# Two-block network on one core: gates of the recurrence split over two levels, norm spreads over the full height, and doubling steps that move only the columns they change

## Chip, cores and metric

One core of a Trainium2 chip. The metric is the device time of one launch in microseconds (us); the median of several runs counts. Everything is float32.

## What is computed

The reference is two transformer blocks behind one another, with 256 tokens of 1024 values. The first block has two layers of a convolutional mixer, cross attention and a feed-forward part (one of them a mixture of eight experts). The second has an attention layer and an RWKV-7 layer, each followed by a squared-ReLU feed-forward part. The change lies in the RWKV layer, whose heart is a recurrence over the tokens, for 16 heads and two directions:

```python
def rwkv7_scan(r, w, k, v, kk, a):
    def step(state, inp):
        r_t, w_t, k_t, v_t, kk_t, a_t = inp
        sa = jnp.einsum('bhvk,bhk->bhv', state, -kk_t)
        state = (state * w_t[:, :, None, :] + sa[..., None] * (kk_t * a_t)[:, :, None, :]
                 + v_t[..., None] * k_t[:, :, None, :])
        return state, jnp.einsum('bhvk,bhk->bhv', state, r_t)
```

The keys `kk` are normalised for each head: `kk / max(sqrt(sum(kk * kk)), 1e-12)`. A gate `g = sigmoid(xg @ g1) @ g2` for each direction multiplies the normalised output of the recurrence.

## The kernel before

The network is written engine by engine. Each engine has its own queue, executed in order; semaphores tie them together, and every wait is written out by hand.

The recurrence (`chunks`) doesn't step through tokens. It takes two chunks of 128 tokens (the time tiles, `t` = 0, 1) and solves a triangular system of 128 x 128 for each. It works on eight *pairs* of heads (128 channels), and in each on two directions `d`. The triangular matrix is inverted by doubling in blocks of 64: level `k` (0 to 5) joins blocks of 2^k rows to blocks twice as large. A pair has four such matrices for each direction (two tiles, two heads, index `n`), and each consists of two corners `b` in the two halves of the partitions. Two kinds of the inverse are kept, itself and its transpose, side by side in one tile `XX` of 2 x 4 x 64 columns: the regions.

A level of one direction goes like this:

- `halves` (L3783): TensorE multiplies `GM` by the kind-0 part of `XX`, eight matmuls of 64 x 64 by 64 columns, into bank `A(d)`.
- `take_half` (L3602): ScalarE copies the 256 columns of the product to `Pb`.
- `steps` (L3796): TensorE multiplies with `Pb`, for both kinds (only kind 1 in level 5), sixteen matmuls of 64 x 64 by 64 columns.
- `step` (L4069): VectorE copies what is fresh into `XX` with `copy_predicated`. In a level only every second block of 2^k columns changes, in kind 0 the even ones and in kind 1 the odd ones; the views `moved` and `places_of` pick these 128 columns of each region, in runs of 2^k, from `XX` and from the result in PSUM.

Each float32 matmul appears in the trace as two records. TensorE's queue runs level by level and, in it, direction 0 and then 1: half products, a filler, steps. The filler is other work of the pair: transposed rows and the Gram products `rest` (L3730, L3733) in levels 1 and 2, the `gates` (L3745, L3746) of both tiles in level 3, nothing in level 4, and the right-hand sides (L3770, L3771) in level 5. Then come the two substitutions (`solve_first`, `carry`, `solve_second`, `state`, `right_sides`, `outputs`), between them the first products of the next pair (`m1`, `gram`).

```python
for d in range(2):
    halves(i, k, d)
    ...
    elif k == 3:
        gates(i, d)
    elif k == LEVELS - 1:
        right_sides(i, 0, d)
    steps(i, k, d)
```

VectorE's queue (`pair`) puts between the levels' steps, in a fixed order, the masking of the Gram products (`keep_rest`, L4061), the pieces of `factors(i + 1)`, which make the operands of the next pair (L3983 to L4004), and the pieces of `output(i - 1)`, which finish the former pair (L4019 to L4045). The product L4002 in `factors` waits until the gates of this pair are done, since it overwrites `rkd`, which they read. ScalarE's queue has `take_half` of each level and between them the exponentials of the next pair, the gates' copy (`take_gates`, L3612) and the normalisation of the former pair (`normalise`, L3618, four for each direction; that of direction 1 stands ahead of level 5). GpSimd makes the reciprocal roots for it.

Ahead of the recurrence, `gates_and_keys` spreads the inverse norms of the 16 heads to all channels. `outof` is a matrix of 16 rows (heads) by 1024 columns, and `scale` has the 16 x 256 inverse norms: eight matmuls (L3390) with 16 rows, each of 256 moving columns, into five banks in turn. VectorE multiplies each by its keys (L3409) and then makes the operands of the first pair for both directions (L3211 to L3218). Behind the spreads TensorE runs the 16 matmuls of the gates' first factor (L3393), and ScalarE applies the sigmoid (L3402). The stage ends, for all engines, with the last of them.

Of the kernel before, what the change touches and what calls it, by code (L numbers as in the profile page):

```python
# [24 lines left out]
P = 128  # L25
SEQ = 256
# [3037 lines left out]
def rwkv_constants():  # L3064
# [17 lines left out]
    rows_of_heads = np.ascontiguousarray(heads_of_rows.T.reshape(KC, P, D // HEAD).transpose(1, 0, 2))  # L3082
    return {"kept_places": np.stack(keep).astype(np.float32), "level_places": np.stack(level).astype(np.int32),
# [3 lines left out]
class Rwkv:  # L3087
# [50 lines left out]
    def place_low(self, ctx):  # L3138
# [3 lines left out]
        self.outof = tmp(ctx, "out_of_heads", [D // HEAD, D])  # L3142
# [77 lines left out]
    def project(self, gain):  # L3220
        m = self.m
        nc, x = m.nc, m.xT
        with ExitStack() as inner:
# [4 lines left out]
            scale = tmp(inner, "scale", [D // HEAD, SEQ])  # L3228
# [57 lines left out]
            def clear_state(pool):  # L3286
                for d in range(2):
                    pool.memset(self.S0[d][:], 0.0)
                pool.memset(self.gn_eps[:], GN_EPS).then_inc(self.cleared.sem, 1)
# [21 lines left out]
            self.low_rank(mixed[0], self.a1, a_low, ACT.Copy, self.a2, "a0", self.rate, mixing(5, mixed[1]), scale=scale)  # L3311
# [3 lines left out]
    def low_rank(self, x, w1, low, func, w2, bias, dst, extra, squares=None, scale=None):  # L3315
# [7 lines left out]
        with m.block() as block:  # L3323
# [20 lines left out]
            def _(act):  # L3344
# [3 lines left out]
                if scale is not None:  # L3348
                    act.wait_ge(summed.sem, summed.at(1))
                    act.activation(scale[:], ps[0:D // HEAD, 1, 0:SEQ], ACT.Sqrt).then_inc(rooted.sem, 1)  # L3350
# [8 lines left out]
            def _(dve):  # L3359
                extra(dve, chain)  # L3360
                if scale is not None:
                    dve.wait_ge(rooted.sem, rooted.at(1))
                    chain.link(dve.tensor_scalar(scale[:], scale[:], 1e-12, None, ALU.max))
                    dve.reciprocal(scale[:], scale[:]).then_inc(inverted.sem, 1)
# [11 lines left out]
    def gates_and_keys(self, x, g1, low, k, scale, kk, places):  # L3376
# [39 lines left out]
    def chunks(self, ctx, y, into, gain, loads):  # L3416
# [82 lines left out]
        def both_kinds(d):  # L3499

            return ps[:, A(d):B(d) + 1, :].rearrange("p a b -> p (a b)")[:, 4 * HEAD:]

        def made(d, kind, n):

            at = n * HEAD
            if region(kind, d):
                return ps[:, B(d), at:at + HEAD]
            return ps[:, A(d), 4 * HEAD + at:4 * HEAD + at + HEAD]
# [39 lines left out]
        with m.block() as block:  # L3548
# [14 lines left out]
            def _(pool):  # L3563
# [655 lines left out]
```

## Time and profile before

| | |
|---|---|
| median of 3 runs | 2555.06 us (2554.2 to 2559.51) |
| the profiled execution | 2555.09 us, span 2553.4 us |
| TensorE (PE), busy share of the span | 96% |
| TensorE weight loads (PEld) | 83% |
| VectorE (DVE) | 43% |
| ScalarE (ACT) | 19% |
| GpSimd (POOL) | 7% |
| stage of gates and keys | about 2030 to 2044.5 us |
| recurrence, eight pairs | about 2045 to 2313 us |

The profile comes from one execution. A row of the timeline has the start in us from the span's start, the time from the first start to the last end of the merged instructions, engine, line, operation, the tiles (out<-in), shapes and count, and in brackets the idle time of the engine before it with what ended it. A matmul's shape is "stationary rows*columns moving". A row of the windows has the window and its length, then busy us and instructions of PE, PEld, DVE, ACT and POOL, then the granted share of TensorE's clock (1.00 is 2.4 GHz, 0.50 is 1.2 GHz), the DMA share and GB/s. A row of the waits has the waiting instruction, what it waited for, us in total, times and the longest. A row by line and shape has the count, busy us and mean ns of one, then idle time before.

### The profile page before, as it was taken

The numbers are of one execution on the slowest core, as the hardware profiler recorded it, in microseconds if no ns is written. First come the engines' busy times: TensorE is split into PE (matmuls) and PEld (weight loads), VectorE is DVE, ScalarE is ACT, GpSimd is POOL, SyncE is SP. The second block draws the span as 40 slices with busy tenths as digits, with TensorE's granted clock in tenths as the row PEclk, the third lists the DMA queues.
The fourth block names the chain that finished last, engine by engine and source line by source line (L and its number), as shares of the span: only waits on it lengthen the run. The fifth ranks groups of instructions, "written<-read, shape, count | busy, mean of one in ns | idle before, by whom it ended". The sixth has DMA issues, their size and how long they took to land. (4 is left out here: it accounts for less than half of the span.)

```text
span 2553.4 us, 80275 instructions
## 1 busy us (share of the span) xinstructions
PE 2461.7 (96%) x36143; PEld 2113.9 (83%) x36143; DVE 1086.1 (43%) x2659; ACT 477.5 (19%) x1062; POOL 179.1 (7%) x225
## 2 busy tenths in 40 slices
PE   9999999999999999999999999999999989989998
PEld 7898878789879989999999898777768777778775
DVE  5672554477321010110101102446664478866666
ACT  2112000211132323210000001310010455542000
POOL 0100000010022322210000000000000001110000
PEclk9999999999999999999999999999999999989999
DMA  7444554554589999999999999326565000020453
GB/s 239 156 143 144 170 164 132 170 180 149 203 312 407 407 407 408 407 407 405 407 407 407 407 407 341 112 90 201 202 204 167 1 9 8 7 71 26 167 178 116
DMA packets 289906, 571.11 MB, mean 224 GB/s; under 512 B 18190, under 2 KB 180244, under 8 KB 289764
## 3 DMA queue, kind: packets, MB, share of 16 engines
q1 hardware_dynamic: 289764, 569.10, 61.1%
q8 instruction: 103, 1.69, 0.3%
q14 instruction: 39, 0.32, 0.0%
HBM read 567.98 MB, written 5.28 MB: 225 GB/s over the span
## 5 line engine op out<-in xcount | busy, mean ns | idle before, releaser
L2688 PE MATMUL ps<-xg,ring 128*64 128x80 f32 x14336 | 507.5, 233 | 7.0 <-issue 5.6
L2688 PEld LDWEIGHTS ps<-xg,ring 128*64 128x64 f32 x14336 | 500.9, 137 | 12.3 <-issue 8.5
L2811 DVE TENSOR_TENSOR hidden<-acted,ps 128x320 f32<-128x320 f32 x64 | 28.5, 446 | 659.8 <-PE ps L2688 659.8
L2704 PE MATMUL ps<-hidden,expert_down 128*64 128x80 f32 x7168 | 257.8, 234 | 9.3 <-issue 3.9
L2704 PEld LDWEIGHTS ps<-hidden,expert_down 128*64 128x64 f32 x7168 | 252.7, 138 | 11.7 <-issue 8.9
L2753 ACT ACTIVATE ring<-second 128x1792 f32<-128x1792 f32 x60 | 101.9, 1698 | 210.0 <-PE ps L2688 190.9
L639 PE MATMUL ps<-xT,ring 128*128 128x256 f32 (+1 forms) x592 | 131.4, 381 | 0.4 <-PEq L474 0.4
L639 PEld LDWEIGHTS ps<-xT,ring 128*128 128x128 f32 (+1 forms) x592 | 105.9, 181 | 23.7 <-issue 3.5
L2745 POOL COPY ring<-second 128x1792 f32<-128x1792 f32 x60 | 100.9, 1681 | 307.9 <-PE ps L2688 183.8
L639 PE MATMUL ps<-ring,xT 128*128 128x256 f32 (+1 forms) x544 | 108.9, 361 | 2.2 <-PEq L1144 2.2
L639 PEld LDWEIGHTS ps<-ring,xT 128*128 128x128 f32 x544 | 96.0, 190 | 14.5 <-issue 3.0
L2046 PEld LDWEIGHTS ps<-xT,ring 128*128 128x128 f32 x720 | 87.4, 192 | 14.3 <-issue 9.1
L2081 PE MATMUL ps<-ring,hidden 128*128 128x512 f32 x192 | 92.9, 593 | 0.0
L2046 PE MATMUL ps<-xT,ring 128*128 128x128 f32 x720 | 90.2, 275 | 0.4 <-DVE made L2165 0.4
L2760 ACT ACTIVATE acted<-ps 128x320 f32<-128x320 f32 x64 | 22.4, 401 | 353.9 <-PE ps L2688 353.5
L2016 ACT ACTIVATE S<-u 128x512 f32<-128x512 f32 x8 | 5.0, 630 | 392.2 <-DVE u L2221 389.2
L1763 PE MATMUL ps<-ring,hidden 128*128 128x512 f32 x176 | 77.2, 592 | 0.0
L1047 DVE SCALAR_TENSOR_TENSOR conv<-gated,cols,conv 128x256 f32<-128x256 f32 x180 | 71.4, 477 | 0.0
L2081 PE MATMUL ps<-wT,hS 128*128 128x512 f32 x128 | 65.4, 593 | 0.0
L639 PE MATMUL ps<-second,ring 128*128 128x256 f32 x288 | 63.8, 379 | 0.0
L1763 PEld LDWEIGHTS ps<-ring,hidden 128*128 128x128 f32 x176 | 32.7, 190 | 37.3 <-issue 37.3
L2046 PE MATMUL ps<-T,S 128*128 128x128 f32 x480 | 63.4, 275 | 0.0
(662 smaller groups left out, 3929.1 us busy)
## 6 DMA issues: line engine op xcount, KB each, us to landing
expert_down<-in_moe_w_down_dram SPq DMA_DIRECT2D x96, 1024.0 KB, 16.8
ring<-in_mlp_w_dram SPq DMA_DIRECT2D x64, 1024.0 KB, 5.4
ring<-in_moe_w_gate_dram SPq DMA_DIRECT2D x68, 896.0 KB, 15.9
ring<-in_moe_w_up_dram SPq DMA_DIRECT2D x68, 896.0 KB, 16.4
second<-in_moe_w_gate_dram SPq DMA_DIRECT2D x30, 1792.0 KB, 17.4
second<-in_moe_w_up_dram SPq DMA_DIRECT2D x30, 1792.0 KB, 18.8
ring<-in_w_xkv_dram SPq DMA_DIRECT2D x16, 1024.0 KB, 5.5
expert_down<-in_moe_w_down_dram SPq DMA_DIRECT2D x32, 512.0 KB, 16.2
```

The lines of the kernel that those rows point to most:

```text
L639: mm = pe.matmul(bank(n, dst), left(here), right(here), start=(i == 0), stop=(i == len(pairs) - 1))
L1047: ins = dve.scalar_tensor_tensor(conv[:, i, :], gated[:, i, k:k + SEQ], w, conv[:, i, :], ALU.mult, ALU.add)
L1763: mm = pe.matmul(ps[:, 4 + 2 * t + half, :], hidden[:, p, f, t * P:(t + 1) * P], w[:, f, half * 512:(half + 1) * 512], start=first and f = ...
L2016: act.activation(junk[:, 0:512], half_of(dst, t, half), ACT.Square, accum_out=part[:, t, half:half + 1]).then_inc(squares_summed.sem, 1)
L2046: mm = pe.matmul(to, left[:, c, :], right[:, c, :], start=(c == 0), stop=(c == H - 1))
L2081: return pe.matmul(to, left, right, start=first, stop=last, skip_group_check=True)
L2688: mm = pe.matmul(bank[b][o:o + HEAD, at, :], w[:, c, f * P + o:f * P + o + HEAD], xg[:, p * E_STEP + c, :], start=(p == 0 and c == 0 and a ...
L2704: mm = pe.matmul(yT[c // 4][o:o + HEAD, c % 4, :], w[:, j, c * P + o:c * P + o + HEAD], hidden[:, f, :], start=False, stop=False, skip_gro ...
L2745: pool.tensor_copy(self.expert_in(1, p), self.expert_waiting(1, p, 1)).then_inc(loaded[1][p], 16)
L2753: act.activation(self.expert_in(0, p), self.expert_waiting(0, p, 1), ACT.Copy).then_inc(loaded[0][p], 16)
L2760: act.activation(acted[:, part, :], src, ACT.Silu).then_inc(act_done, 1)
L2811: dve.tensor_tensor(hidden[:, part, :], acted[:, part, :], src, ALU.mult).then_inc(hidden_ready, 1)
```

## The change

- The gates of a direction are split by time tile: tile 0 is the filler of level 3, tile 1 that of level 4.
- `halves` moves only the 32 columns of each 64 that the level changes, and its results are packed (32 columns for each matrix). `take_half` copies 128 columns instead of 256 and writes them, in runs of 2^k, to the changing places of `Pb`; the rest of `Pb` is cleared once, by GpSimd, ahead of the first pair. `steps` moves 32 columns as well; its results are packed, 128 for each kind, and VectorE reads them contiguously. The stationary operands keep their 64 columns.
- The normalisation of direction 1 is cut in two parts, which stand behind level 4's first copy and between the copies of the gates; the gates' copies move between the copies of levels 4 and 5.
- The norm spreads take all 128 rows: `outof` and `scale` get 112 rows of zeros. They no longer stand ahead of the gates' matmuls but between them, one behind each from the fifth of direction 0 to the fourth of direction 1.

```diff
@@ gates_and_keys, tensor
-                for c in range(KC):
-                    if c >= SPREAD:
-                        pe.wait_ge(taken.sem, taken.at(c - SPREAD + 1))
-                    pe.matmul(ps[:, 3 + c % SPREAD, 0:SEQ], self.outof[:, c * P:(c + 1) * P], scale[:], start=True, stop=True).then_inc(spread.sem, 1)
                 for d in range(2):
                     for c in range(KC):
                         mm = pe.matmul(ps[:, 2 * d, 0:SEQ], g1[:, c, d, :], x[:, c, :], start=(c == 0), stop=(c == KC - 1))
+                        if d == 0 and c >= 4:
+                            e = c - 4
+                            pe.matmul(ps[:, 3 + e, 0:SEQ], self.outof[:, e * P:(e + 1) * P], scale[:], start=True, stop=True).then_inc(spread.sem, 1)
+                        elif d == 1 and c < 4:
+                            e = c + 4
+                            if e >= SPREAD:
+                                pe.wait_ge(taken.sem, taken.at(e - SPREAD + 1))
+                            pe.matmul(ps[:, 3 + e % SPREAD, 0:SEQ], self.outof[:, e * P:(e + 1) * P], scale[:], start=True, stop=True).then_inc(spread.sem, 1)
@@ chunks
+        PART = HEAD // 2
-        def both_kinds(d):
-            return ps[:, A(d):B(d) + 1, :].rearrange("p a b -> p (a b)")[:, 4 * HEAD:]
+        def both_kinds(d, k):
+            packed = ps[:, A(d):B(d) + 1, :].rearrange("p a b -> p (a b)")[:, 12 * PART:20 * PART]
+            return packed.rearrange("p (r n m b) -> p r n m b", r=2, n=4, b=1 << k)
+        def changing(block, k, kind, d):
+            return block.rearrange("p (m z b) -> p m z b", z=2, b=1 << k)[:, :, region(kind, d), :]
@@ gpsimd
+                pool.memset(Pb[0][:], 0.0)
+                pool.memset(Pb[1][:], 0.0).then_inc(self.cleared.sem, 1)
@@ scalar, take_half
-                    act.activation(Pb[d][:].rearrange("p a b -> p (a b)"), ps[:, A(d), 0:4 * HEAD], ACT.Copy).then_inc(q["half_ready"].sem, 1)
+                    to = changing(Pb[d][:].rearrange("p a b -> p (a b)"), k, 0, d)
+                    act.activation(to, ps[:, A(d), 0:4 * PART].rearrange("p (m b) -> p m b", b=1 << k), ACT.Copy).then_inc(q["half_ready"].sem, 1)
@@ scalar, pair
-                    take_halves(i, 4)
-                    for d in range(2):
-                        take_gates(i, d)
+                    take_half(i, 4, 0)
                     if not first:
-                        normalise(i - 1, 1)
-                    take_halves(i, 5)
+                        normalise(i - 1, 1, range(2))
+                    take_half(i, 4, 1)
+                    take_gates(i, 0)
+                    if not first:
+                        normalise(i - 1, 1, range(2, 4))
+                    take_half(i, 5, 0)
+                    take_gates(i, 1)
+                    take_half(i, 5, 1)
@@ tensor, halves
-                            mm = pe.matmul(ps[other, A(d), n * HEAD:(n + 1) * HEAD], GM[d][h, n, 0, h], XX(i, d, 0, n)[h], start=True, stop=True)
+                            mm = pe.matmul(ps[other, A(d), n * PART:(n + 1) * PART], GM[d][h, n, 0, h], changing(XX(i, d, 0, n)[h], k, 0, d), start=True, stop=True)
@@ tensor, steps
-                                mm = pe.matmul(made(d, kind, n)[on], p if kind else xt, xt if kind else p, start=True, stop=True)
+                                mm = pe.matmul(made(d, kind, n)[on], p if kind else xt, changing(xt if kind else p, k, kind, d), start=True, stop=True)
@@ tensor, pair
-                            elif k == 3:
-                                gates(i, d)
+                            elif k < LEVELS - 1:
+                                gates(i, k - 3, d)
@@ vector, step
-                    x, fresh, places = moved(XXs[d][i % 2][:], k), moved(both_kinds(d), k), places_of(k)
+                    x, fresh, places = moved(XXs[d][i % 2][:], k), both_kinds(d, k), places_of(k)
```

## Rows read from the trace of the kernel before

**Rows 1.** Busy time by window: one middle pair of the recurrence.
```profile
2144.70:2176.80 32.10, 29.39 (x759) 24.47 (x759) 25.75 (x80) 17.94 (x54) 3.25 (x8) 1.00 0.03 7
```

**Rows 2.** Who waited for whom, in the same pair.
```profile
ACT Pb L3602 <- PE ps L3783: 9.9, 8, 1.7
...
DVE XX L4069 <- PE ps L3796: 0.7, 2, 0.5
```

**Rows 3.** Timeline of TensorE, levels 3 and 4 of that pair.
```profile
2153.43 0.63 PE L3783 MATMUL ps<-XX,GM 64*64 64x64 f32 x16
...
2157.55 0.63 PE L3783 MATMUL ps<-XX,GM 64*64 64x64 f32 x16
...
2158.67 0.27 PE L3796 MATMUL ps<-Pb,XX 64*64 64x64 f32 x2 [0.49 <-ACT Pb L3602]
...
2160.83 0.63 PE L3783 MATMUL ps<-XX,GM 64*64 64x64 f32 x16
```

**Rows 4.** Timeline of ScalarE, same pair, level 5.
```profile
2160.69 1.43 ACT L3618 ACTIVATE o<-o,rs 128x64 f32<-128x64 f32 x4
...
2162.01 0.38 ACT L3602 ACTIVATE Pb<-ps 128x256 f32<-128x256 f32 x1
```

**Rows 5.** Timeline of VectorE, same pair, levels 1 to 4.
```profile
2148.45 0.72 DVE L4069 COPY_PREDICATED XX<-level,ps 128x256 f32<-128x256 int32 x1
...
2154.71 0.95 DVE L4061 TENSOR_TENSOR GM<-ps,keep 128x768 f32<-128x768 f32 x1
...
2155.85 0.43 DVE L4069 COPY_PREDICATED XX<-level,ps 128x256 f32<-128x256 int32 x1 [0.19 <-PE ps L3796]
...
2157.22 0.41 DVE L3997 TENSOR_TENSOR front<-r,front 128x256 f32<-128x256 f32 x1
...
2157.90 0.43 DVE L4069 COPY_PREDICATED XX<-level,ps 128x256 f32<-128x256 int32 x1 [0.27 <-issue]
...
2158.97 0.42 DVE L4004 TENSOR_TENSOR front<-kd,eB 128x256 f32<-128x256 f32 x1
...
2159.91 0.43 DVE L4069 COPY_PREDICATED XX<-level,ps 128x256 f32<-128x256 int32 x1 [0.53 <-PE ps L3796]
```

**Rows 6.** Timeline of TensorE outside the recurrence, for the spacing of matmuls.
```profile
86.75 1.03 PE L639 MATMUL ps<-xT,ring 128*64 128x256 f32 x4
...
87.71 2.44 PE L955 MATMUL ps<-vnorm,wsT 128*128 128x64 f32 x20
...
2401.55 1.61 PE L2046 MATMUL ps<-xT,ring 128*128 128x128 f32 x13
```

**Rows 7.** Groups by line and shape, recurrence: a ScalarE copy of 128 elements.
```profile
L3624 ACT ACTIVATE rhs<-ps 64x128 f32<-64x128 f32 x32 | 8.7, 271 | 22.0 <-PE ps L3775 21.6
```

**Rows 8.** Timelines of TensorE, VectorE and ScalarE, stage of gates and keys.
```profile
2029.99 5.66 PE L3390 MATMUL ps<-scale,out_of_heads 16*128 16x256 f32 x16 [1.14 <-PEq L3323]
...
2035.69 0.48 DVE L3409 SCALAR_TENSOR_TENSOR xT<-k,cols,ps 128x256 f32<-128x256 f32 x1 [0.37 <-PE ps L3390]
...
2040.57 0.41 DVE L3218 TENSOR_TENSOR front<-dn 128x256 f32<-128x256 f32 x1
...
2044.15 0.38 ACT L3402 ACTIVATE g_low<-ps 128x256 f32<-128x256 f32 x1 [3.07 <-PE ps L3393]
```

**Rows 9.** Busy time by window again, for the granted clock (PEclk).
```profile
918.80:922.20 3.40, 3.40 (x58) 3.40 (x56) 0.00 (x0) 0.00 (x0) 0.00 (x0) 0.50 1.04 412
...
2031.50:2038.40 6.90, 6.90 (x18) 4.99 (x17) 5.92 (x16) 4.27 (x11) 0.00 (x0) 0.51 0.00 0
...
2161.20:2164.70 3.50, 2.68 (x74) 2.13 (x69) 3.36 (x12) 2.38 (x8) 0.00 (x0) 1.00 0.00 0
```

**Rows 10.** Timeline of TensorE, last pair, half products of levels 2, 3, 5.
```profile
2282.85 0.56 PE L3783 MATMUL ps<-XX,GM 64*64 64x64 f32 x12 [2.54 <-issue]
...
2285.12 1.06 PE L3783 MATMUL ps<-XX,GM 64*64 64x64 f32 x16
...
2297.44 0.79 PE L3783 MATMUL ps<-XX,GM 64*64 64x64 f32 x16
```

More of the change, by code:

```diff
@@ L3141, in place_low @@
         self.into = tmp(ctx, "into_heads", [P, KC, D // HEAD])
-        self.outof = tmp(ctx, "out_of_heads", [D // HEAD, D])
+        self.outof = tmp(ctx, "out_of_heads", [P, D])
         self.loaded = self.m.sig("rwkv_tables_loaded")
@@ L3227, in project @@
             w_low, a_low = tmp(inner, "w_low", [P, SEQ]), tmp(inner, "a_low", [P, SEQ])
-            scale = tmp(inner, "scale", [D // HEAD, SEQ])
+            scale = tmp(inner, "scale", [P, SEQ])
+            by_head = scale[0:D // HEAD, :]
             def mixing(n, dst):
@@ L3288, in clear_state @@
                     pool.memset(self.S0[d][:], 0.0)
+                pool.memset(scale[:], 0.0)
                 pool.memset(self.gn_eps[:], GN_EPS).then_inc(self.cleared.sem, 1)
@@ L3349, in _ @@
                     act.wait_ge(summed.sem, summed.at(1))
-                    act.activation(scale[:], ps[0:D // HEAD, 1, 0:SEQ], ACT.Sqrt).then_inc(rooted.sem, 1)
+                    act.wait_ge(self.cleared.sem, self.cleared.at(1))
+                    act.activation(scale, ps[0:D // HEAD, 1, 0:SEQ], ACT.Sqrt).then_inc(rooted.sem, 1)
                 act.wait_ge(low_done.sem, low_done.at(1))
@@ L3362, in _ @@
                     dve.wait_ge(rooted.sem, rooted.at(1))
-                    chain.link(dve.tensor_scalar(scale[:], scale[:], 1e-12, None, ALU.max))
-                    dve.reciprocal(scale[:], scale[:]).then_inc(inverted.sem, 1)
+                    chain.link(dve.tensor_scalar(scale, scale, 1e-12, None, ALU.max))
+                    dve.reciprocal(scale, scale).then_inc(inverted.sem, 1)
                     dve.wait_ge(self.cleared.sem, self.cleared.at(1))
@@ L3612, in take_gates, with normalise @@
                     act.activation(gb(i, d)[:], ps[:, G(d), 0:SUMS + 4], ACT.Copy).then_inc(q["gates_ready"].sem, 1)
-                def normalise(j, d):
+                def normalise(j, d, ns=range(4)):
                     wait(act, "gn_rstd", j, d + 1)
                     ov = o[d][:].rearrange("p (n e) -> p n e", n=4)
-                    for n in range(4):
+                    for n in ns:
                         a = act.activation(ov[:, n, :], ov[:, n, :], ACT.Identity, bias=rs[d][:, 2, n:n + 1], scale=rs[d][:, 1, n:n + 1])
-                    a.then_inc(q["normed"].sem, 1)
+                    if n == 3:
+                        a.then_inc(q["normed"].sem, 1)
                 def take_right(i, s, d):
@@ L3693, in _ @@
                     take_m1(0, d)
+                act.wait_ge(self.cleared.sem, self.cleared.at(2))
                 for i in range(pairs):
@@ L3739, in rows, with gates @@
                     mm.then_inc(q["rows_done"].sem, 1)
-                def gates(i, d):
-                    wait(pe, "slice_loaded", i, 32)
-                    wait(pe, "rest_kept", i, 2 + d + 1)
-                    for t in range(TT):
-                        pe.matmul(ps[:, G(d), t * P:(t + 1) * P], g_low[:, d, t * P:(t + 1) * P], g2[:, d, :], start=True, stop=True)
-                        mm = pe.matmul(ps[:, G(d), SUMS + 2 * t:SUMS + 2 * t + 2], rkd[d][:, t, :], head_of, start=True, stop=True)
-                    mm.then_inc(q["gates_done"].sem, 1)
+                def gates(i, t, d):
+                    if t == 0:
+                        wait(pe, "slice_loaded", i, 32)
+                        wait(pe, "rest_kept", i, 2 + d + 1)
+                    pe.matmul(ps[:, G(d), t * P:(t + 1) * P], g_low[:, d, t * P:(t + 1) * P], g2[:, d, :], start=True, stop=True)
+                    mm = pe.matmul(ps[:, G(d), SUMS + 2 * t:SUMS + 2 * t + 2], rkd[d][:, t, :], head_of, start=True, stop=True)
+                    if t == TT - 1:
+                        mm.then_inc(q["gates_done"].sem, 1)
                 def values(i, t, hh):
```

9 lines of the change are left out of this document (5 added, 4 removed).

## Prediction

> **What bounds the kernel now.** I read the busy shares by stage first. In one pair of heads of the recurrence (32.1 us, eight of them) TensorE is busy 29.4 us and VectorE 25.8 us, the clock full [rows 1]. So TensorE looks like the bound; the waits of the same pair correct that. ScalarE waits 9.9 us for the half products, which costs nothing by itself, and VectorE waits for a level's step only 0.7 us in all [rows 2]. Both queues are nearly full at once, and the question is which of them a faster level would still meet.
>
> The queue of TensorE shows where a level's time goes. A half-level is: half products of one direction, filler, steps. In level 3 it takes 2.06 us (2153.43 to 2157.55 for two); the filler is the gates of both time tiles. In level 4 there is no filler, the engine idles 0.49 us for ScalarE's copy, and a half-level takes 1.64 us (2157.55 to 2160.83). The gates of a direction thus take 2.06 - 1.64 + 0.49 = 0.91 us [rows 3]. ScalarE adds a delay at level 5: four normalisations (2160.69, 1.43 us) stand ahead of the copy of the half product, which can only follow them at about 2162.0 [rows 4], though that product, begun at 2160.83, was there 0.5 us earlier. VectorE meanwhile works almost without a pause from 2148.45 on: before the steps of levels 3 and 4 it idles 0.19 and 0.53 us, and before the step at 2157.90 another 0.27 us (the product ahead of it ended at 2157.22 + 0.41 = 2157.63) [rows 5].
>
> **Gates by time tile.** One tile of gates takes half of 0.91 us, and with ScalarE's copy now shorter (below) a half-level with it is about 1.65 us in both levels. TensorE is offered 2 x 0.41 = 0.8 us in level 3 and loses nothing in level 4, where the 0.49 us gap is its cover [rows 3]. If the copy were no cover, level 4 would pay the 0.8 us back.
>
> **Half products and steps.** Each product keeps its stationary operand of 64 columns and moves 32 instead of 64. What spaces the products is the load of that operand: twenty matmuls with 128 stationary and 64 moving columns take 2.44 us, less some 0.275 us for the last one (2.44 - 0.275)/19 = 0.114 us apart, and thirteen with 128 moving columns take 1.61 us, (1.61 - 0.275)/12 = 0.111 us apart [rows 6]. Half the moving columns bought nothing there. I take the spacing as unchanged, a gain of zero. The bound on the other side is that the spacing is halved: 0.2 us for each of ten half products and eight steps of a pair, 3.6 us; VectorE would not let that through (below).
>
> A rule bears on this. "TensorEngine Tiling (Array Packing)", section Instruction Overhead, in the Trainium skill says that a matmul with very few moving columns takes as long as one with about sixty. By the rule as by the rows the sum has no gain here; they differ in the cause, and rows 6 show the cause at 128 columns.
>
> ScalarE's copy of a half product shrinks from 256 to 128 elements for each partition: 0.38 us now [rows 4], 271 ns for 128 elements [rows 7], so 0.11 us off each half-level in which it is waited for (levels 3 to 5, six of them): 0.6 us offered, of which the gates' filler hides half. Its output is now in runs of 2 to 16; between 271 and 380 ns I take 271, its own element count. Splitting the second normalisation puts two of its four parts behind level 4: the copy at level 5 comes 0.7 us earlier [rows 4].
>
> The step's source becomes contiguous, its destination stays in runs. At level 1 (runs of two) the copy takes 0.72 us, at levels 3 and 4 0.43 us [rows 5]. If the source was the cause, VectorE gains up to 0.29 us twice in a pair, 8 x 0.3 = 2.4 us after cover; if the destination, nothing. I take nothing, for the destination's runs remain, and keep 2.4 us for the range.
>
> **What VectorE lets through.** So TensorE is offered some 1.2 us in a pair. Now VectorE's queue, in which nothing is removed. The product of kept places at 2154.71 depends on level 2, unchanged. The next step can follow it after about 0.88 us, at 2155.60 instead of 2155.85. Of the 2.05 us from there to the step at 2157.90, some 0.33 us are the wait for level 3's second steps, which now come 0.8 us earlier; 1.72 us are queue, so that step comes at 2157.33. Then stand three products for the next pair; the first of them waits until the gates of direction 0 are done, for it overwrites what they read. Those now end in level 4: half products at 2153.43 + 2 x 1.65 = 2156.7, and behind their 0.56 us the gates, until about 2157.8. The product wanted to start at 2157.67, so 0.2 us are given back. The step behind them starts 0.52 us after the last one ended (2158.97 + 0.42 against 2159.91) [rows 5], a wait on VectorE's own product, and that stays. Gain: 0.57 - 0.2 = 0.37 us. From there to the state's update VectorE has no pause, and TensorE's further lead is lost in waiting for it. Six middle pairs give 6 x 0.37 = 2.2 us. The bound below: if the 0.52 us shrink with the step coming early, 0.5 us more for each.
>
> The first pair has no output of a former pair beside it, so VectorE holds less back: between 0.37 and 1.2 us, I take 0.6 us. The last has no factors of a next one, TensorE bounds it, and part of it ran at half clock: 1.2 us offered, I take 1.5 us (0.8 to 2.5).
>
> **Norm spreads.** They run now as 16 records with 16 rows, 5.66 us from 2029.99, and the gates' 32 records behind them end at about 2044.1 [rows 8], with half of this stretch at half clock [rows 9]. At full clock records of 256 columns come (1.03 - 0.38)/3 = 0.217 us apart [rows 6], 48 of them in 10.4 us. If the full height keeps the clock, TensorE is through at 2040.4. But the eighth spread becomes record 40 of 48 and lands at 2029.99 + 40 x 0.217 + 0.1 = 2038.8, where VectorE takes it at 2035.69 today. Its last product starts 4.88 us and ends 5.29 us after that [rows 8], now at 2044.1. The stage ended with ScalarE's sigmoid at 2044.15 + 0.38 = 2044.53. So 0.4 us are gained of 3.7. The price: TensorE is idle for 4 us from then on. Idle stretches are where the clock went down: after the 2.54 us stall at 2280.3 it was half for 13.7 us [rows 9, 10]. The first pair would begin at half clock. The shortest stretch at 0.50 is 3.4 us [rows 9], and half of its work is lost, 1.7 us; a stretch of twice that costs 3.4 us, none costs nothing. I take 1.5 us, by the shortest.
>
> The cleared buffers (two small memsets on POOL, one on POOL before) and the waits on them end long before they are asked for; nothing, since POOL idles in that stage.
>
> **Sum.** 2.2 + 0.6 + 1.5 + 0.4 - 1.5 = 3.2 us less. The profiled execution took 2555.09 us around a span of 2553.4 and agrees with the median of 2555.06, so 2551.9 us. About 0.2% (5.1 us) is what a measurement of this kernel can tell from no change. Its own range is 2544 to 2556.
>
> **Rival 1, the clock falls in the levels (slower).** The granted clock was 0.51 from 2031.5 to 2038.4, and the engine had been at the 16-row spreads, back to back, before and in it [rows 8, 9]. So an engine that is busy all the time with small products can still be granted 1.2 GHz. Products that move 32 columns behind a 64-column load fill the array half as long, exactly in levels 4 and 5, where there are gaps besides. Price: in the last pair the way from level 3's to level 5's first half product took 2285.12 to 2297.44, 12.3 us, against 7.4 us [rows 3, 10]: 4.9 us for 13.7 us of low clock, 0.36 us for each. One stretch of 7 us, as that at 2031.5, costs 2.5 us; in seven pairs 17.5 us, with the sum 2555.1 - 3.2 + 17.5 = 2569 us; with 3.4 us stretches 2560, with long ones 2586. It decides once the clock falls in more than two pairs. Against it: the emptiest stretches of the levels today (2161.2 to 2164.7) hold the full clock [rows 9]. Chance 0.38.
>
> The Trainium skill, "TensorE: Matmul & The Clock Gate", Part 1, says that the clock follows how busy the engine has recently been. By that rule a full queue of halved products keeps 2.4 GHz and this rival falls; the row of the 16-row spreads disagrees with it, and I follow the row.
>
> **Rival 2, the queue of VectorE gives more.** The level 1 copies get faster, or the 0.52 us wait shrinks, or the halved products do space closer: 3.2 + 2.4 + 2 + 1 gives 2546.5 us. For it: VectorE is what bounds the middle pairs, so each tenth of a microsecond there counts eightfold. Against it: no row shows the source to be the cause. Chance 0.22.
>
> **Rival 3, no more than noise.** VectorE's new wait for the gates is as long as what it gains, the first pair loses what the last wins: 2555 us. Chance 0.12, beside 0.28 for the forecast.
>
> **The numbers.** The forecast's own case is mostly within 0.2% (two thirds), one third faster; rival 3 is within; rival 2 is faster; rival 1 slower with a tenth of it hidden in the gain. That gives faster 0.32, same 0.31, slower 0.37. No sign holds most of it. The range leaves out the best of rival 2 and the worst of rival 1: 2545 to 2573.
>
> **What would show it.** In the changed kernel a half-level of levels 3 and 4 of about 1.65 us on TensorE, the half products' span still 0.6 us (0.4 would refute the load as the bound), ScalarE's copy at 0.27 us, level 1's copy still 0.72 us, a first wait of VectorE on the gates, the period of a middle pair 31.7 us. The stage of the gates ends with VectorE and TensorE idle before it. A granted clock under 1 between 2046 and 2280 would be rival 1 and refute the forecast.

## The result, and the profile after

The changed kernel takes 2563.34 us (median of 15 runs, 2560.14 to 2578.8) against 2555.57 us for the kernel before beside it (15 runs): ratio 1.0041, 95% interval 1.0028 to 1.0054. It is slower, by 0.3% by the two medians and by 0.4% by the ratio on record. The forecast was 2551.9 us, faster; the way of rival 1 came.

The profiled execution took 2575.57 us (span 2573.8 us), 12 us over the median of its own kernel. So how much of it ran at half clock is at the upper end, and the sizes of single stretches below hold for this execution: its mean granted clock was 0.982, that of the median run 0.989. Four of the 15 runs lie at 2574 to 2579 us (this is one of them), the other eleven at 2560 to 2569 us. The page's slices, 64 us each, show where the clock was lower. Counted from one, the recurrence lies in slices 32 to 37:

```profile
PE   9999999999999999999999999899999899999998
...
PEclk9999999999999999999999999999999879989999
```

TensorE's busy tenths give little hint of it. The windows do. The first is the stage of gates and keys, then come the eight pairs, each from its first half product to that of the next (the last to its last half product). The columns are those of [rows 1]; the granted clock is the third from the end:

```profile
2031.80:2048.30 16.50, 12.24 (x48) 10.14 (x48) 10.35 (x28) 6.50 (x14) 0.01 (x1) 0.90 0.00 1
2052.01:2097.24 45.23, 44.40 (x761) 37.51 (x759) 20.37 (x49) 15.85 (x47) 0.00 (x0) 0.58 0.02 5
2097.24:2129.79 32.55, 30.60 (x758) 25.73 (x758) 25.59 (x80) 17.08 (x54) 3.29 (x8) 0.95 0.03 7
2129.79:2161.62 31.83, 29.73 (x758) 24.91 (x758) 25.80 (x80) 17.09 (x54) 3.28 (x8) 1.00 0.03 8
2161.62:2194.55 32.93, 30.81 (x759) 25.74 (x759) 25.61 (x80) 17.10 (x54) 3.28 (x8) 0.95 0.03 7
2194.55:2226.04 31.49, 29.54 (x758) 24.81 (x758) 25.59 (x80) 17.09 (x54) 3.28 (x8) 1.00 0.03 8
2226.04:2257.53 31.49, 29.53 (x758) 24.82 (x758) 25.59 (x80) 17.10 (x54) 3.28 (x8) 1.00 0.03 7
2257.53:2290.09 32.56, 30.60 (x758) 25.62 (x758) 25.58 (x80) 17.10 (x54) 3.28 (x8) 0.95 0.15 47
2290.09:2316.53 26.44, 23.09 (x491) 20.60 (x492) 11.92 (x36) 6.46 (x21) 3.25 (x8) 0.72 0.31 113
```

Read the second number with the clock. At 1.00 a middle pair takes 31.49 us, 0.6 us less than in the kernel before [rows 1]: the change does its work. At 0.95 it is 1 us longer, and the first pair, at 0.58, takes 45.2 us where it took 32.4. From 2049.3 us it ran at half clock for 41.0 us without a break, and was busy for 40.2 of them; then come three stretches of 3.4 us and one of 23.9 us, begun in the last pair. The window of the first:

```profile
2049.30:2090.30 41.00, 40.17 (x633) 33.94 (x624) 18.71 (x44) 12.96 (x38) 0.00 (x0) 0.50 0.03 9
```

Over the recurrence that makes 75.1 us at half clock, against 13.7 us in the kernel before.

The whole difference of the two spans, 20.4 us, by stages: the stage of gates starts 1.8 us later (in the fourteen profiled executions of this document it starts anywhere from 2029.2 to 2032.9 us, also where nothing ahead of it was changed, so this is not laid to the change); from its first product to the first half product 20.25 us instead of 18.06 (+2.2); the first seven pairs 238.1 instead of 225.0 (+13.1); the last pair and all behind it 283.7 instead of 280.3 (+3.4).

### The profile page after: what moved, and what is told of

The parts are those of the page before. It is cut to its first block and busy times, and to the rows that moved or that the text cites. A ratio compares the mean times of both kernels' runs of the same rounds, so it can differ in the third digit from the quotient of the medians.

```text
span 2573.8 us, 80280 instructions
## 1 busy us (share of the span) xinstructions
PE 2486.4 (97%) x36143; PEld 2137.3 (83%) x36143; DVE 1086.0 (42%) x2659; ACT 471.6 (18%) x1062; POOL 180.1 (7%) x228
## 5 line engine op out<-in xcount | busy, mean ns | idle before, releaser
L2046 PEld LDWEIGHTS ps<-xT,ring 128*128 128x128 f32 x720 | 87.3, 192 | 14.6 <-issue 8.8
L3808 PE MATMUL ps<-XX,GM 64*64 64x32 f32 x1280 | 58.0, 234 | 7.4 <-issue 3.1
## 6 DMA issues: line engine op xcount, KB each, us to landing
ring<-in_moe_w_up_dram SPq DMA_DIRECT2D x68, 896.0 KB, 16.6
```

What stands on the lines that cost most here:

```text
L2046: mm = pe.matmul(to, left[:, c, :], right[:, c, :], start=(c == 0), stop=(c == H - 1))
L3808: mm = pe.matmul(ps[other, A(d), n * PART:(n + 1) * PART], GM[d][h, n, 0, h], changing(XX(i, d, 0, n)[h], k, 0, d), start=True, stop=True)
```

## Experiments

The change has three parts that can be made one by one: the **spreads** (full height, put between the gate products), the **gates** (by time tile, with ScalarE's new order) and the **halving** (products that move 32 columns, with their copies). The kernel before ran again beside each group of experiments, with medians of 2554.08 us (e1 to e4), 2556.21 (e5 to e8) and 2555.33 (e9 to e12); each ratio is to the one beside it. The medians are of 10 to 15 runs, but of 5 in e2, 6 in e4 and 7 in e8. "Low" is the time at half clock of the profiled execution from the first product of the recurrence to the end of the last pair; "middle" is the shortest period among the second to the seventh pair; in e4 each of these holds a stretch at half clock, elsewhere the shortest holds none. Both come from one execution: that of e10, 2556.0 us, is 5 us under its median, that of e12, 2558.1 us, 4 us over it.

| kernel | spreads | gates | halving | median us | ratio (95%) | low us | middle us |
|---|---|---|---|---|---|---|---|
| before | old | old | no | 2555.57 | | 13.7 | 32.09 |
| changed | new | new | yes | 2563.34 | 1.0041 (1.0028 to 1.0054) | 75.1 | 31.49 |
| e1 | new | new | no | 2551.20 | 0.9989 (0.9981 to 0.9998) | 10.0 | 31.53 |
| e2 | old | new | yes | 2567.60 | 1.0059 (1.0046 to 1.0072) | 54.6 | 31.48 |
| e3 | old | new | no | 2550.90 | 0.9989 (0.9980 to 0.9997) | 3.4 | 31.54 |
| e4 | old | old | yes | 2570.89 | 1.0063 (1.0049 to 1.0078) | 71.7 | 32.79 |
| e5 | new | new | steps only | 2559.46 | 1.0013 (0.9997 to 1.0029) | 34.1 | 31.54 |
| e6 | new | new | half products only | 2558.55 | 1.0012 (0.9996 to 1.0028) | 6.8 | 31.50 |
| e7 | new | new | yes, with added products | 2570.36 | 1.0054 (1.0035 to 1.0074) | 61.4 | 31.52 |
| e8 | full height, ahead | new | no | 2546.19 | 0.9963 (0.9950 to 0.9976) | 3.4 | 31.53 |
| e9 | new | new | each moved twice | 2552.37 | 0.9989 (0.9980 to 0.9998) | 10.2 | 31.56 |
| e10 | full height, ahead | new | yes | 2560.80 | 1.0021 (1.0010 to 1.0032) | 41.0 | 31.50 |
| e11 | old | split only | no | 2550.34 | 0.9986 (0.9977 to 0.9995) | 3.4 | 31.54 |
| e12 | old | order only | no | 2554.35 | 0.9991 (0.9982 to 1.0000) | 13.7 | 31.74 |

**One part undone or alone (e1 to e4).** e1 takes the halving out of the changed kernel:

```diff
-  pe.matmul(ps[other, A(d), n*PART:(n+1)*PART], GM[d][h, n, 0, h], changing(XX(i, d, 0, n)[h], k, 0, d), ...)
+  pe.matmul(ps[other, A(d), n*HEAD:(n+1)*HEAD], GM[d][h, n, 0, h], XX(i, d, 0, n)[h], ...)
-  pe.matmul(made(d, kind, n)[on], p if kind else xt, changing(xt if kind else p, k, kind, d), ...)
+  pe.matmul(made(d, kind, n)[on], p if kind else xt, xt if kind else p, ...)
```

> The changed kernel with the half products and the steps moving 64 columns again; gates by tile and the norm spreads stay as changed. Theory (the halved moving columns keep the clock of TensorE down once it has fallen): TensorE still idles some 4.3 us ahead of the first pair, so the clock may still fall there, but it comes back within the pair: a first pair of 32 to 36 us instead of 45.2 us, middle pairs of 31.5 to 31.8 us, last pair without the 24 us at half clock; in all about 2551 to 2555 us against 2555.6 us for the kernel before. Rival (the norm spreads alone cause the loss, the width of the moves has no part in it): first pair again about 45 us with some 40 us at half clock, in all about 2563 us.

e2 takes the spreads out, with the 16-row matmuls of before ahead of the gate products.

> The changed kernel with the norm spreads as before (16 rows, all ahead of the gate products); gates by tile and the halved moves stay. Theory (the idle TensorE behind the gate products lets the clock fall, the halved moves keep it down): the fall ahead of the first pair goes, that pair takes 31.5 to 33 us; short stretches at half clock in levels of single middle pairs (1 us each) and the long one in the last pair stay; in all 2551 to 2556 us. Rival (the halved moves alone make the clock fall, wherever they run): the first pair stays near 45 us and the whole near 2563 us.

e3 and e4 put one part alone into the kernel before.

> The kernel before with the gates by time tile and ScalarE's new order alone; spreads and moves as before. Theory: all of the gain of the undisturbed middle pairs comes from here: periods of 31.5 to 31.7 us instead of 32.1 us, no more half clock than in the kernel before, in all about 2551 us. Rival (the gain of the middle pairs comes from the halved copies and products, the gates by tile only put a wait elsewhere): periods of 31.9 to 32.1 us and 2555 us.

> The kernel before with the halved moves alone (half products, steps, ScalarE's copy and the contiguous source of VectorE's copies); spreads and gates as before. Theory: undisturbed middle pairs stay within 0.2 us of 32.1 us since the spacing of the products does not change, but stretches of 3.4 us or more at half clock appear within the levels of middle pairs and the last pair: 2556 to 2562 us. Rival (the halving costs nothing): no such stretches, 2554 to 2555.5 us.

e1 came out as the theory had it, in time and in the first pair, 32.37 us. e2 did not: at 2567.6 us the loss is whole, above the theory's range and above the rival's 2563 us, and the first pair is at 37.8 us between them. So I had given the spreads too much: without the idle stretch that they bring, the clock falls all the same, in five pairs again. Windows of the first four pairs of e2:

```profile
2050.73:2088.52 37.79, 35.49 (x759) 30.51 (x759) 20.23 (x49) 15.72 (x47) 0.00 (x0) 0.77 0.02 7
2088.52:2119.99 31.47, 29.52 (x758) 24.82 (x758) 25.59 (x80) 17.07 (x54) 3.28 (x8) 1.00 0.03 7
2119.99:2152.90 32.91, 30.81 (x758) 25.70 (x758) 25.80 (x80) 17.06 (x54) 3.27 (x8) 0.95 0.03 7
2152.90:2187.34 34.44, 33.14 (x758) 27.89 (x758) 25.60 (x80) 17.07 (x54) 3.27 (x8) 0.85 0.03 7
```

e4 shows it bare, beyond its range of 2556 to 2562 us: of seven periods one is undisturbed, the first, and it is 0.6 us shorter than 32.41 us. All others hold a stretch at half clock. Its first two pairs:

```profile
2051.51:2083.28 31.77, 29.23 (x758) 24.52 (x758) 20.04 (x49) 15.61 (x47) 0.00 (x0) 1.00 0.03 8
2083.28:2117.98 34.70, 32.50 (x758) 27.20 (x759) 25.78 (x80) 16.95 (x54) 3.48 (x8) 0.85 0.03 7
```

What TensorE did before such a fall can be set beside the kernel before. In the second pair of e4 the clock falls at 2100.6 us. Here are the 8 us until shortly before it (from 9.0 to 17.0 us behind the pair's first half product: levels 3 and 4 and the start of level 5), and the same 8 us of a middle pair of the kernel before, where it does not fall:

```profile
2092.28:2100.28 8.00, 6.97 (x226) 6.46 (x222) 7.25 (x25) 4.44 (x17) 2.20 (x6) 1.00 0.08 20
...
2153.71:2161.71 8.00, 7.02 (x228) 6.50 (x224) 6.81 (x25) 4.65 (x16) 1.98 (x6) 1.00 0.08 22
```

TensorE was busy as long in both, 6.97 and 7.02 us, and had as many products; what differs is the columns that the half products and steps moved. The halving makes such a fall likelier, not certain: in e4's own first pair it does not come.

e3 gives the gates the whole of the gain of a middle pair: 31.54 us, where all three parts give 31.49. The six middle pairs make 2.7 us of e3's gain (189.9 instead of 192.6 us), the first pair none (32.37 us). The larger part, 4.7 us, is the last pair and what is behind it (275.6 instead of 280.3 us), with 3.4 us at half clock and not 13.7. The five kernels with split gates and 64 moved columns (e1, e3, e8, e9, e11) have 3.4 or 6.8 us there, the two without the split (before, e12) 13.7 us; why the split shortens that stretch was not followed up.

**How much of the halving (e5, e6).** Against the changed kernel, e5 moves 64 columns in the half products only, e6 in the steps only.

> The changed kernel with the half products alone moving 64 columns again; the steps still move 32. In an undisturbed level the steps carry two products for each one of the half products, so two thirds of the taken-away columns stay away. Theory (the columns moved in the levels decide how easily the clock falls and comes back): less time at half clock than with both halved (62 to 69 us from the first pair on), yet more than with none (0 to 7 us); 2554 to 2562 us. Rival (only the half products matter, since they stand behind a wait): no stretch at half clock in the middle pairs, 2550 to 2552 us.

> The changed kernel with the steps alone moving 64 columns again; the half products still move 32. Theory: one third of the taken-away columns stays away, so at most a stretch or two of 3.4 us in the middle pairs and a shorter one in the last pair: 2551 to 2556 us. Rival (the half products matter alone): the first pair above 40 us and 2560 us or more. If the halved operands of ScalarE and of the products are what gains 0.05 us in an undisturbed middle pair, its period is 31.5 us here too.

Both lie between none and all, at 2559.5 and 2558.6 us. e5 is in its range; e6 is above 2556. The intervals of both reach to 1, so neither is clearly slower than the kernel before. The profiled execution of e6, 2550.3 us, is the fastest of ten that reach to 2569.7 us, so its 6.8 us of low clock are not its usual. Neither group of products decides alone, and the two can't be told apart by these runs.

**Does the clock carry it (e7, e9)?** e7 adds work for TensorE where it waits. `keep_on` is a product of 128 rows by 256 columns that nobody reads; both kernels have one in each pair but the last, behind the second substitution (`solve_second`), and e7 adds two:

```diff
-                def keep_on():
-                    pe.matmul(ps[:, A(0), 0:2 * P], m.ident[:], m.cols[:, 0:2, :], start=True, stop=True)
+                def keep_on(bank=0):
+                    pe.matmul(ps[:, bank, 0:2 * P], m.ident[:], m.cols[:, 0:2, :], start=True, stop=True)
...
                             steps(i, k, d)
+                            if k > 3 and d == 1:
+                                keep_on(C(0))
```

> The changed kernel with one more product of 128 rows by 256 columns behind the steps (4,1) and (5,1) of each pair, into a bank that nobody reads at that time, where TensorE waits for VectorE 0.2 us and 0.7 us anyway. Nothing else changes. Theory (the halved moves act through the clock alone): the short stretches at half clock in the middle pairs and the long one in the last pair go; the first pair, whose fall comes ahead of it, is shorter than 45 us; in all 2551 to 2558 us though TensorE has more to do. Rival (the time at half clock is a symptom of the waits and not their cause): the same stretches and 2565 us or more, by the 0.2 to 0.4 us that the added products take in each pair.

It did not help: 2570.4 us, with windows as these (the first and the third pair):

```profile
2049.88:2089.53 39.65, 38.24 (x762) 31.82 (x762) 20.13 (x49) 15.74 (x47) 0.00 (x0) 0.74 0.02 6
2121.06:2158.02 36.96, 35.75 (x762) 29.55 (x762) 26.17 (x80) 17.09 (x54) 3.28 (x8) 0.82 0.03 7
```

TensorE is busy 96 to 97% of both and is granted 0.74 and 0.82 of its clock. Taken alone this run speaks for its rival: filling the waits of levels 4 and 5 does not hold the clock. e9 puts the question otherwise. It leaves the queue alone and changes what each product moves and, not shown in this excerpt, where it stands in PSUM: its results take the places of 64 columns again, of which ScalarE and VectorE read the first 32.

```diff
+        def twice(cols):
+            p, m_, b_ = cols.shape
+            return cols.unsqueeze(1).to_broadcast([p, 2, m_, b_])
-  ... GM[d][h, n, 0, h], changing(XX(i, d, 0, n)[h], k, 0, d), ...
+  ... GM[d][h, n, 0, h], twice(changing(XX(i, d, 0, n)[h], k, 0, d)), ...
-  ... p if kind else xt, changing(xt if kind else p, k, kind, d), ...
+  ... p if kind else xt, twice(changing(xt if kind else p, k, kind, d)), ...
```

> The changed kernel with each half product and each step moving its 32 changing columns twice, into the 64 columns that the kernel before writes; ScalarE and VectorE read the first 32. Products, waits, operands and the readers' sizes are those of the changed kernel, only the number of columns that TensorE moves is that of the kernel before. Theory (fewer moved columns lower the clock, nothing else of the halving costs): time at half clock from the first pair on falls from 65 to 70 us to under 10 us, undisturbed middle pairs stay at 31.5 us, in all 2550 to 2553 us as with the wide moves (2551.2 us). Rival (the strided operands or the layout in the banks cost, or the data that is moved decides): low clock and time as in the changed kernel, 2560 us or more.

2552.4 us, as expected; 10.2 us at half clock are left (3.4 us ahead of the first pair, 6.8 us in the last), none in between. Windows of its first pair and of a middle one:

```profile
2051.66:2083.70 32.04, 29.71 (x758) 24.70 (x758) 20.06 (x49) 15.65 (x47) 0.00 (x0) 1.00 0.03 7
...
2210.65:2242.21 31.56, 29.87 (x758) 24.82 (x759) 25.62 (x80) 17.11 (x54) 3.28 (x8) 1.00 0.03 7
```

Timeline of TensorE in that middle pair, the half products of two half-levels:

```profile
2222.78 0.63 PE L3813 MATMUL ps<-XX,GM 64*64 64x64 f32 x16
...
2224.39 0.63 PE L3813 MATMUL ps<-XX,GM 64*64 64x64 f32 x16
```

Sixteen records take 0.63 us whether they move 64 columns or 32 (2206.62, below). The same data moved a second time costs 0.07 us in a middle pair, and the kernel is 11 us faster for it. That rules out the strides of the operands, the number of elements that the readers take, the waits, the order of the queue and the data. What lowered the clock is that fewer columns were moved, and written, in the same time. The results of e9 lie 64 columns apart in PSUM and not packed; that the packing has no part in it is therefore not shown. The spans give the price: 2573.8 - 2550.9 = 22.9 us for 75.1 - 10.2 = 64.9 us more at half clock, 0.35 us for each. The other runs say the same without a trace: each has its span and its mean granted clock on record, and twice the missing share of the clock times the span is its time at half clock. Over the 129 runs of the changed kernel and e1 to e12, compared within each kernel, a run with 1 us more at half clock took 0.35 us longer (correlation 0.95).

**The spreads on their own (e8, e10).** In the changed kernel and in e1 the last spread comes late and VectorE ends the stage. e8 keeps the full height and puts the spreads back ahead of the gate products; the moves are wide:

```diff
                 pe.wait_ge(inverted.sem, inverted.at(1))
+                for c in range(KC):
+                    if c >= SPREAD:
+                        pe.wait_ge(taken.sem, taken.at(c - SPREAD + 1))
+                    pe.matmul(ps[:, 3 + c % SPREAD, 0:SEQ], self.outof[:, c * P:(c + 1) * P], scale[:], start=True, stop=True).then_inc(spread.sem, 1)
```

> The kernel before with gates by time tile, and with the norm spreads at full height (128 rows) but still all ahead of the gate products; moves of 64 columns. Theory: the spreads keep the clock up, so the stage of spreads and gate products takes 8 x 0.43 us and then 16 x 0.43 us at full clock, about 10.9 us between its first product and the first products of the recurrence's stage plus 0.8 us, instead of 14.9 us; VectorE has its spreads early and stays off the path. In all 2547 to 2549 us, 2 to 4 us under the kernel with gates by tile alone (2550.9 us). Rival (VectorE's products behind the spreads end the stage whatever TensorE does): the stage stays above 14 us and the whole at 2551 us.

> The kernel with full-height norm spreads all ahead of the gate products (2546.2 us with wide moves), with the halved moves added. Here TensorE neither idles 4 us nor runs at half clock ahead of the first pair. Theory (the halved moves lower the clock in the levels by themselves, even when nothing ahead has lowered it): stretches at half clock in several pairs, 2552 to 2562 us. Rival (the halving is harmless as long as nothing lowers the clock ahead of the first pair): 2545.5 to 2547 us, with 31.5 us for a middle pair.

e8 is the best kernel of the study, 2546.2 us, a little under what was expected; the stage is as expected (2031.45 to 2043.22, 11.8 us). Timeline of TensorE, from the first spread to the first half product:

```profile
2031.45 3.81 PE L3394 MATMUL ps<-scale,out_of_heads 128*128 128x256 f32 x16 [1.15 <-PEq L3326]
2035.09 7.07 PE L3397 MATMUL ps<-mixed,g 128*128 128x256 f32 x32
2043.22 1.16 PE L3721 MATMUL ps<-front 64*64 64x64 f32 x64 [1.06 <-PEq L3387]
...
2046.39 0.68 PE L3793 MATMUL ps<-XX,GM 64*64 64x64 f32 x16 [0.30 <-DVE GM L4066]
```

The spreads take 3.81 us instead of 5.66 and the gates start 3.6 us after them, not 5.6 [rows 8]; TensorE idles 1.06 us and not four. To the first half product it is 14.94 us instead of 18.06. With the seven pairs (222.3 instead of 225.0) and the end behind them (275.8 instead of 280.3, with 3.4 us of low clock in the last pair and not 13.7), less a start that came 1.5 us later, that is the 8.9 us by which the spans of e8 and the kernel before differ. e10 then adds the halving to it and is in its theory's range: 14.6 us slower, and more low clock in pairs that nothing had disturbed ahead. The halving needs no idle stretch of 4 us before it to do harm.

**Which half of the gates (e11, e12).** e11 splits TensorE's gates and leaves ScalarE's order; e12 the other way round.

> The kernel before with TensorE's gates by time tile alone; ScalarE keeps its old order (both gate copies behind the half copies of level 4, then the four parts of the norm). Theory (both halves of the edit are needed: the gates of the second tile come later, and ScalarE would wait for them ahead of the half copies of level 5): periods of undisturbed middle pairs between 31.6 and 32.1 us. Rival (the split alone gives the gain, because it takes 0.4 us off both half-levels of level 3): 31.5 us as with both.

> The kernel before with ScalarE's new order alone; TensorE does both tiles of the gates in level 3 as before. Theory (the new order frees the half copies of level 4 and 5 from gate copies and norm work, 0.4 to 0.6 us in front of them): part of the gain, periods of 31.7 to 32.0 us. Rival (TensorE's split is all): 32.1 us as before; the other way round, 31.5 us with the order alone.

The split alone gives 31.54 us, all of it, so my theory on e11 falls and its rival holds: ScalarE's order adds nothing once the gates are split. Alone, the order gives 31.74 us, in the range of its theory. The two gains, 0.55 and 0.35 us, do not add up (both together, e3, give 0.55), so they seem to be the same one, reached from two sides; which copy brings it was not read from a trace. By the whole time e12 is hardly told from the kernel before (interval to 1.0000).

## Why the prediction was wrong, step by step

**The spacing and the level (right).** Timeline of TensorE in the undisturbed pair from 2194.55, levels 4 and 5, to be read beside [rows 3]:

```profile
2206.62 0.63 PE L3808 MATMUL ps<-XX,GM 64*64 64x32 f32 x16
...
2208.21 0.63 PE L3808 MATMUL ps<-XX,GM 64*64 64x32 f32 x16
...
2209.80 0.63 PE L3808 MATMUL ps<-XX,GM 64*64 64x32 f32 x16
```

Timeline of VectorE in the same pair, beside [rows 5]:

```profile
2198.26 0.73 DVE L4094 COPY_PREDICATED XX<-level,ps 128x256 f32<-128x256 int32 x1
...
2207.07 0.42 DVE L4094 COPY_PREDICATED XX<-level,ps 128x256 f32<-128x256 int32 x1
2207.83 0.48 DVE L4027 SCALAR_TENSOR_TENSOR front<-r,cols,kd 128x256 f32<-128x256 f32 x1 [0.34 <-PE ps L3770]
...
2209.16 0.44 DVE L4094 COPY_PREDICATED XX<-level,ps 128x256 f32<-128x256 int32 x1 [0.17 <-DVE front L4029]
```

The span of the half products is the old one, so the moved columns don't set it. That the load of the stationary operand does, as I took it, fits this, but no run changed that operand by itself. A half-level is 1.59 us (foretold 1.65). The level 1 copy stays at 0.73 us though its source is contiguous now. So the source was not its cost; what is left in runs of two is the destination, as I took it, and the mask (`places`). ScalarE's copy of the half product, in its timeline:

```profile
2210.49 0.28 ACT L3620 ACTIVATE Pb<-ps 128x128 f32<-128x128 f32 x1 [0.38 <-PE ps L3808]
```

0.28 us as taken from [rows 7].

**What VectorE lets through (right in kind, too small).** The step at 2207.07 stands 12.52 us after its pair's start, the one before 13.19 (2157.90 - 2144.71): 0.67 us gained, foretold 0.57. The new wait on the gates is there, 0.34 us, foretold 0.2. The step behind it stands at 14.61 us instead of 15.20, for the 0.53 us ahead of it shrank to 0.17, which I had held fixed and kept as a bound. So 0.6 us in a pair and not 0.37. Two pairs of the eight, the third and the fourth, gain only 0.2 to 0.3 us in every kernel with the split gates (31.88 us in e3); I did not follow up why. So the six middle pairs give 2.7 us without low clock (e1), where the sum had 2.2. The first pair gains the foretold 0.6 us in e4, where it is undisturbed; that comes from the halved products and copies, for with the gates alone (e3) it gains 0.04 us, and with the gates, the copies of 128 elements and products of 64 columns (e9) 0.4 us. In the changed kernel it was never seen undisturbed.

**The norm spreads (half right).** TensorE in the changed kernel's stage:

```profile
2031.76 4.08 PE L3393 MATMUL ps<-mixed,g 128*128 128x256 f32 x10 [1.15 <-PEq L3326]
...
2042.15 1.89 PE L3393 MATMUL ps<-mixed,g 128*128 128x256 f32 x8
2048.33 1.26 PE L3736 MATMUL ps<-front 64*64 64x64 f32 x64 [4.29 <-PEq L3387]
```

The 4 us of idle time came (4.29), VectorE ended the stage, and the clock fell behind it. The gain of 0.4 us did not: with no low clock in the stage (e1) it is 14.9 us from the first product to the recurrence's first, as before. In the changed kernel's profiled execution it is 16.6 us, with 3.4 us at half clock from 2032.2 us on. In the kernel before the recurrence began 0.4 us after ScalarE's last sigmoid (2044.53 to 2044.89), in the changed kernel 0.7 us after VectorE's last product, which starts at 2047.23 and takes 0.41 us; I had ended both stages with the work and left out what follows it. What the step missed was the better order: e8 earns 3.1 us in the same place.

**The step that failed.** It is the price of the clock. The sum had one term for it, "I take 1.5 us, by the shortest", for a single fall behind the idle stretch, and no term at all for the halved moves, which stood only in rival 1, with a chance of 0.38. The runs put another number there: with the halved moves 75.1 us of the recurrence ran at half clock, with the same columns moved twice (e9) 10.2 us, at 0.35 us for each; by the medians the halving costs 11 us (2563.3 against 2552.4). The median run fits: at a granted clock of 0.989 some 56 us of it ran at half clock, against some 26 us in the median run of e9 (0.995), and an estimate from these and the 0.35 us is 11 us.

The fall behind the idle stretch alone is 3.4 us long in e1 and costs 0.8 us to the first half product (18.82 us against 18.06), half of the term. In the profiled execution of the changed kernel a fall at the same place lasted 41.0 us, and the first pair took 13 us more than in e1. That length is not the rule for halved moves: in e5, e6 and e7, where some or all of the products are halved, the fall at this place is 3.4 us long too, and more follow later.

The rest of the sum came near, in part by luck. Without the halving the change takes 2551.2 us, 2.9 us less than the kernel before beside it, against a forecast of 3.2 less. But the parts of e1's profiled execution are others than forecast: middle pairs 2.7 us (2.2), first pair 0.04 (0.6), last pair and behind it 3.7 (1.5), the stage 0.8 lost (1.1), and a stage that starts 2.05 us later, which no term had.

Rival 1 had the mechanism and the point at which it decides, more than two pairs (five, with the last, in this execution). Its price, 0.36 us for each us at half clock, is near the measured 0.35 by luck: it set 4.9 us against all 13.7 us of low clock, of which only 12.3 us lay in the stretch that it measured, which gives 0.40 (the 13.7 us are the trace's; [rows 9] has no row of it). What spoke against it, the emptiest windows at full clock in [rows 9], was no evidence: those windows moved 64 columns, and the change was to that very number. What spoke for it, the 16-row spreads, is weaker than it was put: they had run for only 1.5 us when the clock fell, behind 1.14 us of idle time [rows 8], and in the changed kernel, with products of full height there, it falls at the same place too, if only for 3.4 us.

The rule that the clock follows how busy the engine has recently been (the Trainium skill, "TensorE: Matmul & The Clock Gate", Part 1) does not account for this case if busy is read as the profile's busy time. TensorE was busy for 40.17 of 41.00 us at half clock and it did not rise, the first pair of e9 is 93% busy (29.71 of 32.04 us) at 1.00, and ahead of e4's fall it was as busy as in the kernel before, which kept the clock.

## What to carry to other kernels

Small matmuls need not get faster by moving fewer columns (0.63 us for sixteen records with 64 or 32), and in a stretch of such matmuls the columns that look wasted may be what keeps the clock up: read the granted clock beside every period, before and after. Work that feeds another engine's long chain goes ahead of work that nobody waits for: with the spreads ahead at full height, e8 and e10 took 3.1 us less to the first half product than the kernel before and had no low clock on the way. Where two engines' queues are both nearly full, spread the filler work over the levels that have gaps.

## What the runs showed of the hardware

With spreads of 16 rows, back to back, the clock was at half in every execution that has them: for 6.8 us before, for 10.2 us in e2, e3, e4, e11 and e12, all begun within 2 us of the first spread. With 128 rows ahead of the gates (e8, e10) that stage had none. With 128 rows between the gate products it fell at the same place in three executions (changed, e5, e6), for 3.4 us, and in three not (e1, e7, e9); so the height of the spreads or their place bears on how long it stays down, and is not shown to be what starts it. Moving the same 32 columns twice (e9) kept the clock as moving 64 different ones did (e1). How much time runs at half clock differs from run to run where the halving is in: 18.7 us lie between the fastest and the slowest run of the changed kernel, 4.3 us in e8. In the middle pairs of the changed kernel, e2, e4, e5 and e10 every stretch at half clock begins 17 to 21 us behind the pair's first half product, at the end of level 5 or just behind it; in the third pair of e7 it begins at 13.7 us, ahead of where the others fall. That TensorE can be 96% busy at 0.74 of its clock, with products of full height among the small ones (e7), I had not expected; what would have to be added, and where, for the halved kernel to hold its clock was not tried further.
